# Summing one modulation block on VectorE ahead of the input projection of a two-layer diffusion block

## The chip, the cores and the metric

One core of one Trainium2 chip runs the whole kernel. The metric is the device time of one launch in microseconds (us), the median over several runs.

## The reference

Two layers work on 512 latent tokens and 256 context tokens of width 1024. Each layer normalises the tokens, scales and shifts them with a modulation made from a conditioning vector, mixes them (layer 0: windowed attention beside a gated linear attention; layer 1: neighbourhood attention), adds the result through a modulated gate, and does the same around a feed-forward part. What the change touches is the modulation:

```python
ml = (jax.nn.silu(c) @ w_mod[i] + b_mod[i])[:, None, :]
mc = jax.nn.silu(c_ctx) @ w_mod[i] + b_mod[i]
sh1, sc1, gt1, sh2, sc2, gt2 = jnp.split(ml, 6, axis=-1)
csh1, csc1, cgt1, csh2, csc2, cgt2 = jnp.split(mc, 6, axis=-1)
```

Per layer there are six blocks of 1024 columns, so twelve blocks in all, each a product of two vectors (`c` and `c_ctx`, after SiLU) with a 1024x1024 matrix. Block 2 is `gt1` of layer 0, the gate behind the first mixer. It is not needed before that mixer's output is added.

## The kernel before

All products are in fp32 split into a high and a low part (three matmuls for one). Every engine runs its own hand-ordered list of instructions; semaphores join them.

**Weights.** A weight unit is 128x1024 (512 KB) or less. SyncE (SP) loads units in order into a ring `w_raw` of three; ScalarE rounds each to `w_hi` (L841), GpSimd (POOL) subtracts to get `w_lo` (L526), TensorE multiplies. The first units are `v0` (six units: four for the value columns, whose product has eight steps k = 0 to 7, two steps a unit, and two smaller 640-column ones for 160 further columns), then `in0` (thirteen units, the other columns of the input projection, each half for latent and context tokens). SP also issues, at fixed places between units, the loads of modulation rows.

**Modulation rows.** `m` counts rows of 128x1024 of `w_mod`: m = 8b + k is input block k of modulation block b. Each is a 512 KB load. Blocks 0 and 1 (m = 0 to 15) are finished before or during the first `v0` steps. For m < 40 TensorE does the product itself: `modulation_rows` (L1796) waits for the landing of row m and does four matmuls of 128x32 by 128x256, one to each group of 32 partitions; the 32 matmuls of a block show as 64 records. For m >= 40 (blocks 5 to 11) VectorE does it: `add_rows` (L1288 for k = 0, L1291 for the others) multiplies a row by the scalar of each of two vectors ("lanes") and adds it to an accumulator of 128x1024 each, and TensorE then sums over partitions once (`modulation_sum`, L1811), four matmuls a lane. `mod_used` counts rows done by TensorE, `mod_acc` VectorE's operations, `mod_summed` the sums. After either, ScalarE copies the block out of PSUM (`mod_copy`, L853) and TensorE turns it (`modulation_columns`, L1823).

**Places.** Rows m = 16 to 23 (block 2) lie in the eight slots of `mod_early`; rows 24 to 29 take slots 2 to 7 again, so each of these loads waits until its slot was read. Rows 30 to 33 lie in `gate_b[:, 1]`, `xs[:, 0]`, `xs[:, 1]` and `full`. `xs` is also the scratch of the step that makes `h_lo` (L1459, L1466), and would be the accumulator of block 2.

**The order around the change.** SP issues rows 16 to 23 ahead of the last `v0` unit. Ahead of the second `in0` unit (`in0` + 1) it waits until the tokens are ready and loads rows 30 to 33; ahead of the fourth (`in0` + 3) it loads rows 24 to 29, each behind its slot's wait. VectorE, after making `h_lo` and two mask copies (`window_b`, `near_b`), waits for the end of all `v0` products, and then copies `r_tok` and `a_v` out of PSUM. TensorE turns `r_tok` (L2040), VectorE copies the result to `r_t` (L1494, L1495), TensorE meanwhile does the rows of block 2 and then `gla_z` (L2052), which needs `r_t`. Then come the thirteen `in0` units (L1722). In the middle and at the end of each, `in0_step` inserts small work: in the middle of the first rows 24 to 26, two `gla_z` and the columns of block 2; at its end rows 27 to 29; in the second rows 30 to 33. The first five places are

```python
rows = {(0, 0): 3, (0, 1): 3, (1, 0): 2, (1, 1): 2, (2, 0): 2, (2, 1): 2, (3, 0): 2}
```

where (i, 0) is the middle and (i, 1) the end of unit i. `claim` makes TensorE wait until a PSUM bank was read.

Of the kernel before, what the change touches and what calls it, by code (L numbers as in the profile page):

```python
# [187 lines left out]
def late_rows():  # L188

    steps = {(("fi0L", 0), j): [36 + 2 * j, 37 + 2 * j] for j in range(2, 11)}  # L190
    steps |= {(("fo0L", 0), n): [58 + 2 * n, 59 + 2 * n] for n in range(6)}
    steps |= {(("fi0L", 1), j): [70 + 2 * j, 71 + 2 * j] for j in range(9)}
    steps |= {(("fi1L", 0), j): [86 + 2 * j, 87 + 2 * j] for j in range(1, 5)}
    order = list(steps)
    loads = {at: steps[then] for at, then in zip(order, order[1:])}
    loads[("fi0L", 0), 1] = [40, 41]
    loads[("fi1L", 0), 0] = [88, 89]
    del loads[("fi0L", 1), 8]
    return steps, loads
# [38 lines left out]
def build(nc, a, out):  # L238
# [14 lines left out]
    def sp(name):  # L253
        return start[name]
# [7 lines left out]
    with ExitStack() as ctx:  # L262
# [177 lines left out]
        def gate_load(eng, j):  # L440
            eng.wait_ge(gate_out, 16 * (j + 1))
            if j == 1:
                eng.wait_ge(mod_summed, 5)
            if gb_after[j]:
                eng.wait_ge(post_n, gb_after[j])
            else:
                eng.wait_ge(gl_o, NT)
            rows, n = gate_rows[j], 2 if j < 2 else 1
            eng.dma_start(gate_b[:, 0:n], bass.AP(rows.tensor, rows.offset, [[0, P], [D, n], [1, D]]))\
                .then_inc(gate_in, 16)  # L450
# [24 lines left out]
        def lanes(b):  # L475
            return 2 if b < 8 else 1

        def sums_done(m):
            return sum(lanes(x // KT) for x in range(MOD_LATE, m + 1))

        def sum_place(b, lane):
            return (gate_b if b in (6, 8, 9) else xs)[:, 1 if b == 9 else lane, :]
# [1 line left out]
        def mod_load(eng, m):  # L484
            if m >= MOD_LATE:
                if mod_free(m):
                    eng.wait_ge(mod_acc, sums_done(mod_free(m) - 1))
                if m in (43, 91):
                    eng.wait_ge(pre_lo, PRE["mix1"] if m == 43 else PRE["ffn1L"] + LT)
            elif mod_free(m):  # L490
                eng.wait_ge(mod_used, mod_free(m))
            b, k = divmod(m, KT)
            l, i = divmod(b, 6)
            if m < 2 * KT:
                both = a["w_mod"][0, k * P:(k + 1) * P, 0:2 * D].rearrange("p (i h n) -> p i h n", i=2, h=2)
                eng.dma_start(mod_place(m).rearrange("p (i n) -> p i n", i=2), both[:, :, b])\
                    .then_inc(mod_landing(m)[0], 16)
                return
            eng.dma_start(mod_place(m), a["w_mod"][l, k * P:(k + 1) * P, i * D:(i + 1) * D])\
                .then_inc(mod_landing(m)[0], 16)  # L500
# [139 lines left out]
        @block.sync  # L640
        def _(sync):
            sync.dma_start(ident[:], a["k_ident"]).then_inc(ident_in, 16)
            sync.dma_start(par_rows[0:96, 0, :], a["b_mod"].rearrange("l (r n) -> (l r) n", n=P)).then_inc(par_in, 16)
            at = 0
            for name in ("g_mix_pre", "g_mix_post", "g_ffn_pre", "g_ffn_post", "gla_norm_g"):
                src = a[name].rearrange("l (r n) -> (l r) n", n=P)
                n = src.shape[0]
                sync.dma_start(par_rows[at:at + n, 1, :], src).then_inc(par_in, 16)
                at += n
            for src in (a["c"].rearrange("b (r n) -> (b r) n", n=P), a["c_ctx"].rearrange("(r n) -> r n", n=P)):  # L650
                sync.dma_start(par_rows[at:at + KT, 1, :], src).then_inc(par_in, 16)
                at += KT
            sync.dma_start(sink[:], a["a_sink"].partition_broadcast(P)).then_inc(par_in, 16)
            for m in range(KT):
                mod_load(sync, m)
            for u, parts in enumerate(units):
                if u in (sp("v0") + 1, sp("v0") + 2):
                    first = KT + 4 * (u - sp("v0") - 1)
                    for m in range(first, first + 4):
                        mod_load(sync, m)  # L660
                if u == sp("v0") + RAW:
                    for dst, src in ((mask_in[:, 0:LT * 2 * P], a["k_near"]), (mask_in[:, LT * 2 * P:], a["k_window"]),
                                     (tri[:].rearrange("p a n -> p (a n)"), a["k_tri"])):
                        sync.dma_start(dst, src).then_inc(consts_in, 16)
                if u == sp("v0") + RAW + 2:
                    for m in range(2 * KT, 3 * KT):
                        mod_load(sync, m)
                if u == sp("in0") + 1:
                    sync.wait_ge(pre_lo, PRE["mix0"] + NT)
                    sync.wait_ge(mod_turned, 2)  # L670
                    for m in range(3 * KT + 6, 3 * KT + 10):
                        mod_load(sync, m)
                if u == sp("in0") + 3:
                    for m in range(3 * KT, 3 * KT + 6):
                        mod_load(sync, m)
                if u == sp("in0") + 11:
                    sync.wait_ge(gl_q, NT)
                    sync.wait_ge(gl_k, NT)
                    for dst, src in ((cos, a["k_cos"]), (sin, a["k_sin"])):
                        sync.dma_start(dst, src).then_inc(rope_in, 16)  # L680
                if u == sp("out0L") + RAW:
                    gate_load(sync, 0)
                if u >= RAW:
                    sync.wait_ge(w_hi_done, u - RAW + 1)
                    sync.wait_ge(*low_ready(u - RAW))
                for layout, at, width, src in parts:
                    dst = w_raw[{"top": slice(0, 64), "bottom": slice(64, P)}.get(layout, slice(0, P)), u % RAW, :]
                    if layout == "fm":
                        dst = dst.rearrange("p (k n) -> p k n", k=KT)
                        dst = dst[:, :, at:at + width]  # L690
                    elif layout == "four":
                        dst = dst[:, 0:4 * VR].rearrange("p (k n) -> p k n", k=4)[:, :, at:at + width]
                    else:
                        dst = dst[:, at:at + width]
                    sync.dma_start(dst, src).then_inc(landed[u % RAW], 16)
            for t in L_TILES:
                sync.wait_ge(post_x, POST["fo1L"] + t + 1)
                sync.dma_start(out[0, t * P:(t + 1) * P, :], x_res[:, t, :]).then_inc(stored, 16)
            sync.wait_ge(stored, 16 * LT)
# [122 lines left out]
        def _(act):  # L822
# [21 lines left out]

            def mod_copy(b):

                if b < 5:
                    act.wait_ge(mod_used, KT * (b + 1))
                else:
                    act.wait_ge(mod_summed, b - 4)  # L850
                if b >= 2:
                    act.wait_ge(mod_turned, b - 1)
                act.activation(row_place(b), ps(mod_bank(b), 0, 256), ACT.Copy).then_inc(mod_copied, 1)  # L853
# [338 lines left out]
        def _(dve):  # L1192
            def pre_scale(name, i, tiles):
                n = PRE[name] + i
                dve.wait_ge(pre_rs, n + 1)
                if name == "mix1":
                    dve.wait_ge(mod_summed, 6)
                if n >= 2:
                    dve.wait_ge(pre_tr, n - 1)
                dve.tensor_scalar(xs[:, n % 2, :], x_res[:, tiles[i], :], rs_pre[:, n:n + 1], None,  # L1200
                                  ALU.mult).then_inc(pre_xs, 1)
# [73 lines left out]

            def add_rows(at):

                free = {5: (pre_tr, PRE["mix1"]), 6: (post_n, POST["fo0L"]), 7: (mod_summed, 1), 8: (mod_summed, 2),
                        9: (mod_summed, 2), 10: (mod_summed, 3), 11: (pre_tr, PRE["ffn1L"] + LT)}
                for m in late_steps.get(at, ()):  # L1280
                    b, k = divmod(m, KT)
                    dve.wait_ge(*mod_landing(m))
# [201 lines left out]
            dve.wait_ge(consts_in, 16 * 3)  # L1484
            dve.tensor_copy(window_b[:], mask_in[:, LT * 2 * P:])
            dve.tensor_copy(near_b[:].rearrange("p t n -> p (t n)"), mask_in[:, 0:LT * 2 * P]).then_inc(masks_done, 1)
            dve.wait_ge(w_used, sp("v0") + KT // 2 + 2)
            rows = [ps(6 + b, 0, 3 * VR).rearrange("p (t n) -> p t n", t=3) for b in range(2)]
            for b in range(2):
# [211 lines left out]
        def _(pe):  # L1701
# [339 lines left out]
                               r_tok[:, t, :], ident[:], start=True, stop=True)  # L2041
            mm.then_inc(r_turned, 1)
            read_by((2, 6), (r_in, 1))
            modulation_rows(range(2 * KT, 3 * KT))

            def gla_z(n):
                bank, t = 4 + n % 2, GLA_TILES[n]
# [215 lines left out]
```

## Time and profile before

| | us |
|---|---|
| median of 3 runs | 1747.09 |
| lowest, highest | 1743.4, 1752.45 |
| profiled execution, whole | 1751.41 |
| its span | 1749.6 |
| TensorE matmul busy | 1677.9 (96%) |
| VectorE busy | 709.6 (41%) |
| ScalarE busy | 641.9 (37%) |
| GpSimd busy | 678.1 (39%) |

The span is the stretch of the profile in which the engines work; the whole time is 1.8 us more. Matmuls overlap in the pipeline, so a group's busy time is not their sum. All times of the trace are us from the start of the span.

### The profile page before, as it was taken

The numbers are of one execution on the slowest core, as the hardware profiler recorded it, in microseconds if no ns is written. First come the engines' busy times: TensorE is split into PE (matmuls) and PEld (weight loads), VectorE is DVE, ScalarE is ACT, GpSimd is POOL, SyncE is SP. The second block draws the span as 40 slices with busy tenths as digits, with TensorE's granted clock in tenths as the row PEclk, the third lists the DMA queues.
The fourth block names the chain that finished last, engine by engine and source line by source line (L and its number), as shares of the span: only waits on it lengthen the run. The fifth ranks groups of instructions, "written<-read, shape, count | busy, mean of one in ns | idle before, by whom it ended". The sixth has DMA issues, their size and how long they took to land.

```text
span 1749.6 us, 25876 instructions
## 1 busy us (share of the span) xinstructions
PE 1677.9 (96%) x10242; PEld 1397.5 (80%) x10242; DVE 709.6 (41%) x1124; ACT 641.9 (37%) x1118; POOL 678.1 (39%) x454
## 2 busy tenths in 40 slices
PE   6999999999999999999899999999999999999997
PEld 4868887777877887878899878877887888888886
DVE  5135547707589635403455420015771451011103
ACT  4242126726422122213555342236762522222221
POOL 3211222038455545433542043335433444444443
PEclk9999999999999999999999999999999999999999
DMA  9553101023465645524556636432002353333331
GB/s 356 182 169 85 38 25 49 1 81 115 146 188 192 229 145 182 167 87 118 154 160 183 193 107 116 91 98 95 2 2 61 100 165 97 105 90 97 98 98 67
DMA packets 211987, 207.17 MB, mean 118 GB/s; under 512 B 16262, under 2 KB 180636, under 8 KB 211612
## 3 DMA queue, kind: packets, MB, share of 16 engines
q1 hardware_dynamic: 199208, 165.53, 31.6%
q10 hardware_dynamic: 12660, 39.99, 7.4%
q8 instruction: 82, 1.34, 0.3%
q14 instruction: 37, 0.30, 0.1%
HBM read 203.37 MB, written 2.13 MB: 117 GB/s over the span
## 4 chain that ended last, share of the span: by engine, by line
PE 82%; DVE 5%; issue 4%; ACT 4%; POOL 4%; DMA 1%; SPq 0%; ACTq 0%; POOLq 0%; DVEq 0%
PE ps L1722 38%; PE ps L1749 26%; PE ps L1900 3%; POOL w_lo L526 3%; PE ps L1956 3%; PE ps L2016 3%; PE ps L1921 3%; ACT w_hi L841 2%; PE ps L1796 1%; PE ps L1835 1%; DVE xs L1291 1%; DMA w_raw<-in_w_ffn_in 1%; PE ps L1968 1%; DVE hid_f L1310 1%; DMA mod_early<-in_w_mod 1%
## 5 line engine op out<-in xcount | busy, mean ns | idle before, releaser
L526 POOL TENSOR_TENSOR w_lo<-w_raw,w_hi 128x1024 fp32r<-128x1024 f32 (+1 forms) x221 | 558.5, 2529 | 892.4 <-ACT w_hi L841 892.2
L1722 PE MATMUL ps<-h_hi,w_hi 128*128 128x512 f32 (+1 forms) x1488 | 496.9, 352 | 11.9 <-POOL w_lo L526 8.1
L1722 PE MATMUL ps<-h_hi,w_lo 128*128 128x512 f32 (+1 forms) x1488 | 492.4, 349 | 0.0
L1722 PE MATMUL ps<-h_lo,w_hi 128*128 128x512 f32 (+1 forms) x1488 | 491.2, 349 | 0.0
L841 ACT ACTIVATE w_hi<-w_raw 128x1024 fp32r<-128x1024 f32 (+1 forms) x273 | 286.6, 1051 | 346.0 <-PE ps L1749 312.0
L1722 PEld LDWEIGHTS ps<-h_hi,w_hi 128*128 128x128 f32 x1488 | 269.9, 189 | 56.9 <-issue 20.8
L1722 PEld LDWEIGHTS ps<-h_hi,w_lo 128*128 128x128 f32 x1488 | 269.5, 189 | 36.1
L1722 PEld LDWEIGHTS ps<-h_lo,w_hi 128*128 128x128 f32 x1488 | 269.5, 189 | 35.7
L526 DVE TENSOR_TENSOR w_lo<-w_raw,w_hi 128x1024 fp32r<-128x1024 f32 x52 | 69.3, 1335 | 201.7 <-ACT w_hi L841 198.8
L1749 PE MATMUL ps<-w_hi,hid_hi 128*128 128x512 f32 x440 | 137.0, 393 | 8.0 <-ACT mod_row L853 4.2
L1310 DVE TENSOR_TENSOR hid_f<-silu_g,ps 128x512 f32<-128x512 f32 (+1 forms) x66 | 39.3, 595 | 254.2 <-PE ps L1722 253.8
L1749 PE MATMUL ps<-w_lo,hid_hi 128*128 128x512 f32 x440 | 136.1, 391 | 0.0
L1749 PE MATMUL ps<-w_hi,hid_lo 128*128 128x512 f32 x440 | 136.1, 391 | 0.0
L912 ACT ACTIVATE hid_hi<-hid_f 128x512 fp32r<-128x512 f32 (+1 forms) x66 | 37.0, 560 | 252.2 <-DVE hid_f L1310 252.2
L1749 PEld LDWEIGHTS ps<-w_hi,hid_hi 128*128 128x128 f32 x440 | 82.6, 189 | 27.0 <-issue 10.2
L1749 PEld LDWEIGHTS ps<-w_lo,hid_hi 128*128 128x128 f32 x440 | 83.1, 189 | 17.4
L1749 PEld LDWEIGHTS ps<-w_hi,hid_lo 128*128 128x128 f32 x440 | 82.9, 188 | 17.3
L1749 PE MATMUL ps<-w_hi,h_hi 128*128 128x512 f32 x256 | 81.9, 402 | 10.6 <-POOL w_lo L526 3.4
L941 ACT ACTIVATE prob<-prob,negm 128x512 f32<-128x512 f32 (+2 forms) x112 | 78.1, 699 | 27.1 <-DVE negm L1350 18.4
L908 ACT ACTIVATE silu_g<-ps 128x512 f32<-128x512 f32 (+1 forms) x66 | 34.5, 523 | 144.5 <-PE ps L1722 144.4
L1749 PE MATMUL ps<-w_lo,h_hi 128*128 128x512 f32 x256 | 81.1, 399 | 0.0
L1749 PE MATMUL ps<-w_hi,h_lo 128*128 128x512 f32 x256 | 80.4, 396 | 0.0
(223 smaller groups left out, 1898.8 us busy)
## 6 DMA issues: line engine op xcount, KB each, us to landing
w_raw<-in_w_ffn_in SPq DMA_DIRECT2D x132, 512.0 KB, 3.8
w_raw<-in_w_ffn_out SPq DMA_DIRECT2D x66, 512.0 KB, 3.5
mod_raw<-in_w_mod ACTq DMA_DIRECT2D x42, 512.0 KB, 4.5
w_raw<-in_na_w_in SPq DMA_DIRECT2D x32, 512.0 KB, 3.7
mod_early<-in_w_mod SPq DMA_DIRECT2D x30, 512.0 KB, 9.8
full<-in_w_mod ACTq DMA_DIRECT2D x15, 512.0 KB, 5.1
w_raw<-in_ab_w_in SPq DMA_DIRECT2D x18, 256.0 KB, 5.9
w_raw<-in_ab_w_in SPq DMA_DIRECT2D x9, 512.0 KB, 8.9
```

Of the source, the lines that this page charges most:

```text
L526: eng.tensor_tensor(w_lo[:, u % RING, 0:width], w_raw[:, u % RAW, 0:width], w_hi[:, u % RING, 0:width].bitcast(F32), ALU.subtract).then_in ...
L841: act.activation(w_hi[:, u % RING, 0:width], w_raw[:, u % RAW, 0:width], ACT.Copy).then_inc(w_hi_done, 1)
L908: act.activation(silu_g[:, f % 2, 0:width], ps(2 * (f % 2), 0, width), ACT.Silu)\
L912: act.activation(hid_hi[:, j * width:(j + 1) * width], hid_f[:, f % 2, 0:width], ACT.Copy)\
L941: act.activation(prob[:, p % 2, x, 0:n], prob[:, p % 2, x, 0:n], ACT.Exp, bias=negm[:, c % 2, head:head + 1], scale=SCALE if layer == 0 el ...
L1310: dve.tensor_tensor(hid_f[:, f % 2, 0:width], silu_g[:, f % 2, 0:width], ps(2 * (f % 2) + 1, 0, width), ALU.mult).then_inc(ff_full, 1)
L1722: mm = pe.matmul(o[0], sta(x, o), mov(y, o), start=first and n == 0, stop=last and n == 2)
L1749: mm = pe.matmul(o, act(x, k, t), w[y][:, c:c + n], start=k == 0 and (x, y) == ("hi", "hi") and first_in_bank(name, i, c), stop=k == n_uni ...
L1900: mm = pe.matmul(ps(scores_bank(layer, p, x), at, at + width), q, kk[:, col:col + width], start=at % 512 == 0, stop=i == len(runs[x]) - 1, ...
L1921: mm = pe.transpose(ps(4 + x, j * P, (j + 1) * P), probs(p, x, j), ident[:])
L1956: mm = pe.matmul(ps(bank, at, at + P, 64 * x, 64 * x + 64), value_tile(p, x, j), turned_probs(layer, p)[:, x, j * P:(j + 1) * P], start=j ...
L2016: mm = pe.matmul(place(t), h_act(x, k, t), w[y][:, at:at + width], start=k == 0 and (x, y) == ("hi", "hi") and (first or t in (0, 3)), sto ...
```

## The change

Block 2 goes over to VectorE. Its accumulation stands in VectorE's list between the two mask copies and the wait for the end of the `v0` products, TensorE does `modulation_sum(2)` where it did the 32 row matmuls, and the loads of rows 30 to 33 move in SP's list from ahead of `in0` + 1 to ahead of `in0` + 2, behind a wait for that sum, since two of them write where the accumulators lie. The loads of rows 24 to 29 stay ahead of `in0` + 3. The counts that waits use are adapted.

```diff
@@ late_rows
     order = list(steps)
+    steps["v0"] = list(range(2 * KT, 3 * KT))
     loads = {at: steps[then] for at, then in zip(order, order[1:])}
@@ gate_load
-                eng.wait_ge(mod_summed, 5)
+                eng.wait_ge(mod_summed, 6)
@@
+        def by_sums(m):
+            return m // KT == 2 or m >= MOD_LATE
+
         def sums_done(m):
-            return sum(lanes(x // KT) for x in range(MOD_LATE, m + 1))
+            return sum(lanes(x // KT) for x in range(m + 1) if by_sums(x))
+
+        def rows_done(m):
+            return sum(not by_sums(x) for x in range(m + 1))
@@ mod_load
             elif mod_free(m):
-                eng.wait_ge(mod_used, mod_free(m))
+                prev = mod_free(m) - 1
+                eng.wait_ge(*(mod_acc, sums_done(prev)) if by_sums(prev) else (mod_used, rows_done(prev)))
@@ sync
-                if u == sp("in0") + 1:
+                if u == sp("in0") + 2:
                     sync.wait_ge(pre_lo, PRE["mix0"] + NT)
                     sync.wait_ge(mod_turned, 2)
+                    sync.wait_ge(mod_summed, 1)
                     for m in range(3 * KT + 6, 3 * KT + 10):
                         mod_load(sync, m)
                 if u == sp("in0") + 3:
@@ mod_copy
-                if b < 5:
-                    act.wait_ge(mod_used, KT * (b + 1))
+                if b < 5 and b != 2:
+                    act.wait_ge(mod_used, rows_done(KT * (b + 1) - 1))
                 else:
-                    act.wait_ge(mod_summed, b - 4)
+                    act.wait_ge(mod_summed, max(1, b - 3))
@@ pre_scale
-                    dve.wait_ge(mod_summed, 6)
+                    dve.wait_ge(mod_summed, 7)
@@ add_rows
-                free = {5: (pre_tr, PRE["mix1"]), 6: (post_n, POST["fo0L"]), 7: (mod_summed, 1), 8: (mod_summed, 2),
-                        9: (mod_summed, 2), 10: (mod_summed, 3), 11: (pre_tr, PRE["ffn1L"] + LT)}
+                free = {2: (pre_lo, NT), 5: (pre_tr, PRE["mix1"]), 6: (post_n, POST["fo0L"]), 7: (mod_summed, 2),
+                        8: (mod_summed, 3), 9: (mod_summed, 3), 10: (mod_summed, 4), 11: (pre_tr, PRE["ffn1L"] + LT)}
@@ vector
             dve.tensor_copy(near_b[:].rearrange("p t n -> p (t n)"), mask_in[:, 0:LT * 2 * P]).then_inc(masks_done, 1)
+            add_rows("v0")
             dve.wait_ge(w_used, sp("v0") + KT // 2 + 2)
@@ tensor
             read_by((2, 6), (r_in, 1))
-            modulation_rows(range(2 * KT, 3 * KT))
+            modulation_sum(2)
```

## Rows read from the trace of the kernel before

**Rows 1.** The page's first line.
```profile
span 1749.6 us, 25876 instructions
```

**Rows 2.** Chain that ended last, in time order: start, us, what; 90 to 111 us.
```profile
90.51 1.36 PE ps L2040 x11
91.87 3.56 PE ps L1796 x62
95.43 1.91 PE ps L2052 x4
97.34 4.36 PE ps L1722 x24
101.71 1.43 PE ps L1796 x24
...
105.42 4.24 PE ps L1722 x24
109.66 1.43 PE ps L1796 x24
```

**Rows 3.** Timeline of VectorE, 60 to 93 us: start, us, instruction, idle before.
```profile
60.46 0.69 DVE L1486 CAST near_b<-mask_in 128x1024 bf16<-128x1024 f32 x1
89.01 0.42 DVE L1490 COPY r_tok<-ps 128x96 f32<-128x96 f32 x2 [27.87 <-PE ps L2016]
...
92.62 0.40 DVE L1495 COPY r_t<-ps 32x256 f32<-32x256 f32 x1
```

**Rows 4.** Timeline of SP's DMA issues: rows 16-23, 24-29, then a weight unit.
```profile
40.58 7.92 SPq L499 DMA_DIRECT2D mod_early<-in_w_mod  x8
...
93.35 2.96 SPq L499 DMA_DIRECT2D mod_early<-in_w_mod  x6
...
96.94 3.81 SPq L695 DMA_DIRECT2D w_raw<-in_ab_w_in  x1
```

**Rows 5.** Issue to landing: `mod_early`, 40-49 and 93-98 us; the unit of 96.94.
```profile
DMA to landing us min/median/max: 5.4/7.5/9.2
...
DMA to landing us min/median/max: 3.7/7.0/8.9
...
w_raw<-in_ab_w_in SPq DMA_DIRECT2D x1, 512.0 KB, 11.5
```

**Rows 6.** Timeline of TensorE at a later block's sum, two lanes.
```profile
511.05 1.07 PE L1811 MATMUL ps<-xs,one_hot 128*32 128x256 f32 x16 [0.79 <-DVE xs L1291]
```

**Rows 7.** Timeline of VectorE, 465 to 560 us: accumulation of a later block.
```profile
468.78 3.55 DVE L1288 TENSOR_SCALAR xs<-mod_raw,c_pad 128x1024 f32<-128x1024 f32 x2
472.25 2.47 DVE L1291 SCALAR_TENSOR_TENSOR xs<-mod_raw,c_pad,xs 128x1024 f32<-128x1024 f32 x2
...
479.65 4.61 DVE L1291 SCALAR_TENSOR_TENSOR xs<-mod_raw,c_pad,xs 128x1024 f32<-128x1024 f32 x2
```

**Rows 8.** Timeline of GpSimd, some of 59 to 89 us, and one at 480 us.
```profile
59.02 4.38 POOL L526 TENSOR_TENSOR w_lo<-w_raw,w_hi 128x1024 fp32r<-128x1024 f32 x1 [15.79 <-ACT w_hi L841]
...
66.00 1.57 POOL L526 TENSOR_TENSOR w_lo<-w_raw,w_hi 128x640 fp32r<-128x640 f32 x1 [1.08 <-ACT w_hi L841]
...
82.17 2.38 POOL L526 TENSOR_TENSOR w_lo<-w_raw,w_hi 128x1024 fp32r<-128x1024 f32 x1 [5.62 <-ACT w_hi L841]
...
480.04 3.14 POOL L526 TENSOR_TENSOR w_lo<-w_raw,w_hi 128x1024 fp32r<-128x1024 f32 x1 [3.07 <-ACT w_hi L841]
```

**Rows 9.** Timeline of ScalarE at the end of the sixth `v0` step.
```profile
65.18 0.74 ACT L841 ACTIVATE w_hi<-w_raw 128x640 fp32r<-128x640 f32 x1 [5.62 <-PE ps L2016]
```

**Rows 10.** Windows: length, busy (count) of PE, PEld, DVE, ACT, POOL, then PEclk, DMA, GB/s.
```profile
88.99:92.00 3.01, 1.49 (x19) 1.49 (x23) 1.35 (x4) 0.00 (x0) 0.00 (x0) 1.00 0.00 0
...
348.70:352.70 4.00, 2.03 (x26) 1.43 (x26) 2.33 (x7) 2.32 (x6) 0.00 (x0) 1.00 0.00 2
352.70:356.10 3.40, 3.17 (x8) 2.52 (x9) 0.00 (x0) 0.47 (x1) 2.37 (x1) 0.50 0.02 5
...
1366.50:1369.90 3.40, 2.18 (x9) 2.11 (x10) 3.13 (x6) 2.17 (x3) 1.26 (x2) 0.50 0.02 7
1369.90:1373.30 3.40, 3.40 (x9) 2.70 (x8) 1.20 (x4) 1.34 (x4) 1.77 (x1) 0.50 0.06 16
```

## The prediction

> **What bounds the kernel now.** The page gives the frame: a span of 1749.6 us [rows 1], which with the 1.8 us around it is the 1751.4 us of the profiled execution; that is 4.3 us over the median of 1747.1. I work out a difference on the profile's own times and put it on the median.
>
> I then read the chain of waits in order of time around the work that changes. From 90.5 us on it lies on TensorE alone: turning `r_tok`, the rows of block 2 (3.56 us), `gla_z`, half of the first `in0` unit, rows 24 to 26, and so on [rows 2]. So each us that TensorE gains or loses here moves the end by as much, unless a wait for another engine or for a DMA opens.
>
> The timeline of VectorE comes next, because the new work goes there. It finishes `near_b` at 61.15 (60.46 + 0.69) and does nothing until 89.01, where the end of the `v0` products lets it copy `r_tok`; a hole of 27.9 us. Its last copy to `r_t`, which `gla_z` needs, ends at 93.02 (92.62 + 0.40) [rows 3]. Last, the queue of SP with the time from issue to landing: rows 16 to 23 are issued from 40.58 to 48.5, and the longest takes 9.2 us, so all are there before 57.7. Rows 24 to 29 are issued from 93.35 to 96.3, each when TensorE has read its slot, followed by the weight units of `in0` + 3 and + 4 [rows 4, 5].
>
> **The change, part by part.**
>
> *TensorE's product.* Removed: 32 matmuls (64 records), 3.56 us [rows 2]. Added: 8 matmuls, 16 records; such a sum took 1.07 us from its first start to its last end at 511 us [rows 6], and at the pace of the row matmuls (3.56 / 62 = 0.057 us a record) it is 0.92. Starting at 91.87 the sum ends near 92.8. `gla_z` could follow, but `r_t` is ready only at 93.02, so it starts at about 93.05 instead of 95.43. Gain: 2.4 us (bounds 2.0 if the semaphore takes 0.4 us more, 2.6 if nothing but the sum counted). This wait costs 0.25 us and is new.
>
> *VectorE's accumulation.* Added: two operations of the L1288 kind and fourteen of the L1291 kind. A pair of the latter takes 2.47 us undisturbed, 4.61 us when a GpSimd subtraction falls into it; the GpSimd operation of 480.04 then takes 3.14 instead of 2.38 us [rows 7, 8]. So a pair loses 2.14 us to each full unit. For the pair of L1288, 3.55 - 2.14 = 1.41 undisturbed [rows 7]. Work: 1.41 + 7 x 2.47 = 18.7 us. GpSimd has five units in the hole: the one of 59.02 (until 63.4), two of 640 columns (the first of them right behind it, the second at 66.00), and those of 74.17 (like the next) and 82.17 [rows 8]. With 2.14 for a full unit and 1.3 for a 640-column one (1.57 less the share 0.9 = 2.14/2.38, rounded down) the loss is 3 x 2.14 + 2 x 1.3 = 9.0. The end is 61.15 + 18.7 + 9.0 = 88.9 us, just before `r_tok` wants the engine at 89.01. I take no delay; bounds: 6.5 us early, if the GpSimd operations fell only beside dead time, and 1.5 us late.
>
> The Trainium skill's page "SBUF — State Buffer", section "Who interferes with whom", says that a VectorE operation with two SBUF inputs, or in a two-port mode, and a GpSimd operation shut each other out for the whole instruction. The disturbed pair agrees in kind, but lost 2.14 us and not the full 2.38. By the page's rule the loss would be 3 x 2.38 + 2 x 1.57 = 10.3 us and VectorE would end at 90.1, 1.1 us late; by the row it is on time.
>
> *The other side of it.* The `w_lo` of the fourth `v0` unit is done at 63.4. It is used in the seventh `v0` step, which begins just before 65.18, where ScalarE is released by the end of the sixth [rows 9]: at about 64.9. One VectorE operation in front of it costs GpSimd 0.76 us (3.14 - 2.38), which fits into the 1.5 us. I take nothing; two more would cost TensorE up to 1 us. The 640-column unit behind it is needed only after two more steps.
>
> *SP's queue.* This is the costly part. The loads of rows 30 to 33 used to go out during the `v0` products, alone, and had landed long before use. They now wait for the sum: 92.8 us and some 0.13 for the semaphore (row 24 used to be issued 0.13 us after its slot was free), so 92.95. SP takes its list in order, and behind that wait stand the weight unit `in0` + 2, then rows 24 to 29, then `in0` + 3 and + 4. The early reading of `mod_early` by VectorE does not help rows 24 to 29, because SP stands in front of them. Before, row 24 was the first of a burst; now five 512 KB loads are ahead of it. In the burst of before, the first load landed at 93.35 + 3.7 = 97.05, the sixth (row 29) at about 95.9 + 8.9 = 104.8, the eighth (`in0` + 4) at 96.94 + 11.5 = 108.44 [rows 4, 5]. That is 1.55 us a load up to the sixth and 1.63 up to the eighth; the eighth lands 15.1 us after the first issue. In the new order row 24 is sixth, row 25 seventh, row 26 eighth. At the pace of the rows (3.7 + 7 x 1.55 = 14.55) rows 24, 25, 26 land at about 104.4, 105.9 and 107.5. Bounds for the last: 105.95 (as if the weight unit ahead cost nothing, 13.0) and 108.5 (15.1, and half a us for SP).
>
> TensorE would ask for row 24 at 93.05 + 1.91 + 4.36 = 99.3 [rows 2]. It waits 5.3 us, does each row as it comes, and has finished row 26 at 107.5 + 0.48 (a third of 1.43) = 107.95. Before, the same point was 101.71 + 1.43 = 103.14 [rows 2]. Loss against before: **4.8 us**, with the 2.4 us gained already in it (bounds 3.3 and 5.8). Rows 27 to 29 land by 107.5 + 3 x 1.55 = 112.2; TensorE asks for them at 109.66 + 4.8 = 114.4, so there is no second wait. Unit `in0` + 2 lands as the fifth, near 103, and is needed after two whole `in0` units, past 118; `in0` + 3 lands near 113.8, and ScalarE comes to it only after the end of the first unit, 109.66 + 4.8 = 114.5. Both are covered.
>
> *TensorE's clock.* After a stretch in which TensorE was busy 2.03 of 4.0 us the granted clock fell to 0.50 (1.2 GHz) for 3.4 us, at 352.7; at 1366.5 it stayed there for two such stretches, 6.8 us, the first of them busy only 2.18 us [rows 10]. With 1.5 of 3.0 us busy around 89 us it did not fall [rows 10]. The new stretch, 99.3 to 107.9, has some 1.4 us of work in 8.6: less than before either fall. So I expect a fall. It costs half of the time that TensorE works at it: 1.7 us for 3.4 us, up to 3.4 us for 6.8; part of it is spent waiting, so I take 2.4 (bounds 0 and 3.4).
>
> *The rest* (counts in the other waits, `mod_copy(2)` earlier by some 2.5 us, places of the later blocks) moves nothing that is late.
>
> Sum: 4.8 + 2.4 = +7.2 us, in the profile's terms 1751.4 + 7.2 = 1758.6, on the median 1747.1 + 7.2 = **1754.3 us** (+0.4%).
>
> **The rivals.**
>
> *The rows come in time.* If loads did not land in the order of issue, or the queue drained faster than 0.4 us a load, there would be no wait at 99.3 and the gain of 2.4 us remains: 1744.7. For it: nothing else is being loaded then. Against it: in the burst of before the first load landed 3.7 us, the sixth 11.5 us and the eighth 15.1 us behind the first issue. It decides if row 26 lands before 99.3, 6.4 us after SP's wait ends.
>
> *Late rows, but the clock holds.* +4.8: 1751.9. For it: there are three small bursts of rows in the gap. Against it: the falls of before came after less idling.
>
> *Worse in every queue.* Row 26 at the upper bound (+1), VectorE 1.5 us late, a stall of 1 us in the seventh step and the clock at half for 6.8 us (+1): about +11.5, 1758.6. The mechanism that would do it is VectorE overrunning 89.01, since that moves `r_tok`, the sum, SP's wait and the rows together; beyond 1.5 us of overrun the total is over +8.7. The rule of the page "SBUF — State Buffer" of the Trainium skill would give 1.1 us of that overrun, +8.3 in all, 1755.4.
>
> *Every accumulation slow.* If all sixteen ran beside GpSimd as in the disturbed pairs, 8 x 4.61 = 36.9 us from 61.15 would end at 98.0, 9 us late: +16. Only five GpSimd units exist in the hole, which speaks against it.
>
> **How the numbers follow.** About 0.5% (8.7 us) is what a measurement of this kernel can tell from no change. Chances: forecast (late rows and a clock fall, +6 to +9) 0.50; late rows without a fall 0.20; worse in every queue 0.15; rows in time 0.12; all slow 0.03. The three runs of before spread over 9 us, so the median of a few may be off by 2 to 3. Slower by over 0.5%: a quarter of the forecast, most of the two worse cases, 0.29. Faster by over 0.5% needs the rival of -2.4 and a low draw: 0.02. Within: 0.69. The range reaches from the rows in time (1744.7) to somewhat beyond the worse case: 1745 to 1761.
>
> **What would show each step.** In the profile after: sixteen L1288 and L1291 operations from 61.2 to about 89, and `r_tok` at 89.0; L1811 at 91.9 for 1 us; `gla_z` near 93; the four loads issued by SP from about 92.95, followed by a weight unit and then rows 24 to 29; TensorE idle from 99.3 on "DMA mod_early", row 26 done near 107.9; a stretch of half clock behind it; from there on everything later by the same amount. I am wrong if the idle is missing or under 3 us, if VectorE ends after 90.5, or if a later wait swallows the shift.

## The result, and the profile after

| | before | after |
|---|---|---|
| median of 6 runs | 1749.07 us | 1758.11 us |
| lowest, highest | 1743.4, 1752.45 | 1756.52, 1761.5 |
| span of the profiled execution | 1749.6 us | 1756.6 us |

The ratio is 1.0059 (95% interval 1.004 to 1.0078): slower by 7 to 14 us. The forecast was +7.2 us, 1754.3, with 1758.1 inside the range. Three more runs of the kernel before put its median at 1749.07 where the forecast had started from 1747.09; between the two medians above lie 9.0 us.

VectorE first. Its timeline in the changed kernel (start us, us, instruction, idle before) answers to [rows 3]:

```profile
60.16 0.69 DVE L1495 CAST near_b<-mask_in 128x1024 bf16<-128x1024 f32 x1
60.76 4.86 DVE L1297 TENSOR_SCALAR xs<-mod_early,c_pad 128x1024 f32<-128x1024 f32 x2
65.54 22.39 DVE L1300 SCALAR_TENSOR_TENSOR xs<-mod_early,c_pad,xs 128x1024 f32<-128x1024 f32 x14
88.71 0.42 DVE L1500 COPY r_tok<-ps 128x96 f32<-128x96 f32 x2 [0.78 <-PE ps L2026]
```

The sixteen operations fill the hole and end at 87.93, 0.78 us before `r_tok` is due. `r_tok` itself starts at 88.71 against 89.01 before; it starts between 87.7 and 89.3 in the profiles of this study, at 88.74 and 87.95 in two executions of one kernel, so stages are best measured from here.

The chain in order of time (start, us, what) answers to [rows 2]:

```profile
90.21 1.36 PE ps L2050 x11
91.57 1.04 PE ps L1821 x13
92.61 0.02 issue
92.62 0.03 SPq L679
92.65 0.03 issue
92.68 0.34 SPq L507
...
97.36 9.10 DMA mod_early<-in_w_mod
106.46 0.04 issue
106.50 1.08 PE ps L1806 x8
107.58 3.71 PE ps L2062 x4
111.29 0.62 PE ps L1833 x2
111.91 6.33 PE ps L1732 x24
118.24 1.43 PE ps L1806 x24
```

Behind the turning of `r_tok` the chain leaves TensorE, which it did not do in the kernel before [rows 2]: from the sum (L1821) it goes to SP, through the issues of the four loads that waited for it, a weight unit and rows 24 and 25, then the 9.1 us from the issue of row 26 to its landing. The timeline of SP shows the order of the queue, and answers to [rows 4]:

```profile
92.68 0.34 SPq L507 DMA_DIRECT2D gate_b<-in_w_mod  x1
93.07 0.90 SPq L507 DMA_DIRECT2D xs<-in_w_mod  x2
94.01 0.43 SPq L507 DMA_DIRECT2D full<-in_w_mod  x1
94.54 0.61 SPq L704 DMA_DIRECT2D w_raw<-in_ab_w_in  x1
95.20 4.29 SPq L507 DMA_DIRECT2D mod_early<-in_w_mod  x6
```

What TensorE waits for shows in its own timeline:

```profile
104.02 2.28 PE L1806 MATMUL ps<-mod_early,c_pad 128*32 128x256 f32 x16 [4.76 <-DMA mod_early<-in_w_mod]
106.50 1.08 PE L1806 MATMUL ps<-mod_early,c_pad 128*32 128x256 f32 x8 [0.20 <-DMA mod_early<-in_w_mod]
```

4.76 us of waiting for row 24, then the rows one by one as they land. The windows of the same stretch (columns as in [rows 10]) show the clock:

```profile
98.90:102.90 4.00, 0.36 (x3) 0.04 (x1) 0.00 (x0) 0.28 (x1) 0.00 (x0) 0.99 1.06 338
102.90:106.50 3.60, 2.17 (x17) 0.43 (x17) 0.00 (x0) 0.78 (x1) 2.35 (x1) 0.50 1.02 416
106.50:111.90 5.40, 5.40 (x15) 2.05 (x16) 0.00 (x0) 0.00 (x0) 0.00 (x0) 0.50 1.09 363
111.90:116.60 4.70, 4.70 (x17) 3.98 (x16) 2.92 (x6) 0.00 (x0) 0.00 (x0) 0.52 0.72 178
116.60:120.00 3.40, 3.40 (x35) 2.15 (x34) 0.00 (x0) 1.72 (x3) 0.00 (x0) 1.00 0.00 0
```

The clock falls to half at 102.9 and is back at 116.6, 13.7 us later, though TensorE has worked without a break since 106.5. After the first rows TensorE does the same work as before in more time: `gla_z` 3.71 us against 1.91, the columns 0.62 against 0.37, half a unit 6.33 against 4.24 [rows 2]; together +4.1 us. The stage ends where the state products begin (L2084 before, L2094 after). The rows of these lines (durations in ns, first and last start in us) put them at 157.1 in the kernel before, 68.1 us behind `r_tok`, and at 165.7 in the changed one:

```profile
L2084 PE MATMUL ps<-b_v,kg_t x176: 268/270/321, 157.1 to 185.2; 64*64 64x128 f32 x176
L2094 PE MATMUL ps<-b_v,kg_t x176: 268/270/321, 165.7 to 193.8; 64*64 64x128 f32 x176
```

That is 77.0 us behind `r_tok`. So the stage is 8.9 us longer: 4.74 us until row 26 is done (107.58 - 88.71 = 18.87 against 103.14 - 89.01 = 14.13), and 4.14 of half clock behind it. The first part has some half clock in it too: row 26 alone took 1.08 us, where a single row takes 0.64 at full clock (in the run with 11 filling matmuls below), so of the 8.9 us some 4.3 are late rows and 4.6 the clock.

The span grew by only 7.0. The last operation of L941 (L950 in the changed kernel) starts at 1305.2 before and 1314.9 after, 9.7 us later; the last table load of L908 (L917) at 1379.0 and 1385.9, 6.9 us later. Between the two the kernel before has its 6.8 us at half clock (1366.5 to 1373.3 [rows 10]), and the changed one, in this execution, has no such stretch. That fits the 2.8 us; half clock far behind the change comes and goes from one execution to the next (the second profile of the kernel with rows first has such stretches near 268 and 351 us, the first has none there), and the stage is the better measure of the change.

### The profile page after: what moved, and what is told of

The parts are those of the page before. It is cut to its first block, busy times and chain, and to the rows that moved or that the text cites. A ratio compares the mean times of both kernels' runs of the same rounds, so it can differ in the third digit from the quotient of the medians.

```text
span 1756.6 us, 25804 instructions
## 1 busy us (share of the span) xinstructions
PE 1678.5 (96%) x10194; PEld 1395.1 (79%) x10194; DVE 733.6 (42%) x1140; ACT 642.2 (37%) x1118; POOL 679.9 (39%) x454
## 4 chain that ended last, share of the span: by engine, by line
PE 84%; DVE 5%; issue 4%; POOL 3%; ACT 3%; DMA 1%; SPq 1%; ACTq 0%; DVEq 0%; POOLq 0%
PE ps L1732 40%; PE ps L1759 26%; PE ps L1910 3%; PE ps L2026 3%; PE ps L1966 3%; POOL w_lo L534 2%; PE ps L1931 2%; DMA mod_early<-in_w_mod 1%; PE ps L1845 1%; ACT w_hi L850 1%; PE ps L1806 1%; DVE xs L1300 1%; PE ps L2121 1%; PE ps L1978 1%; DVE full L1249 1%
## 5 line engine op out<-in xcount | busy, mean ns | idle before, releaser
L1759 PEld LDWEIGHTS ps<-w_lo,hid_hi 128*128 128x128 f32 x440 | 83.4, 189 | 17.5
L950 ACT ACTIVATE prob<-prob,negm 128x512 f32<-128x512 f32 (+2 forms) x112 | 78.2, 699 | 28.5 <-DVE negm L1359 19.6
L917 ACT ACTIVATE silu_g<-ps 128x512 f32<-128x512 f32 (+1 forms) x66 | 34.5, 523 | 145.1 <-PE ps L1732 144.8
```

The source lines that it names most:

```text
L917: act.activation(silu_g[:, f % 2, 0:width], ps(2 * (f % 2), 0, width), ACT.Silu)\
L950: act.activation(prob[:, p % 2, x, 0:n], prob[:, p % 2, x, 0:n], ACT.Exp, bias=negm[:, c % 2, head:head + 1], scale=SCALE if layer == 0 el ...
L1759: mm = pe.matmul(o, act(x, k, t), w[y][:, c:c + n], start=k == 0 and (x, y) == ("hi", "hi") and first_in_bank(name, i, c), stop=k == n_uni ...
```

## The experiments

Seven runs of six kernels were made, in two sets, each beside the kernel before. The table sets the times beside the stage, `r_tok` to first state product, from each profile; the ratio of the changed kernel is that of the result above.

| kernel | ratio to before (95%) | `r_tok` | first state product | stage |
|---|---|---|---|---|
| before | | 89.01 | 157.1 | 68.1 |
| changed | 1.0059 (1.0040 to 1.0078) | 88.71 | 165.7 | 77.0 |
| rows 24 to 29 first | 1.0002 (0.9988 to 1.0016) | 88.74 | 154.6 | 65.9 |
| the same again | 0.9987 (0.9972 to 1.0002) | 87.95 | 153.8 | 65.9 |
| move of the loads alone | 1.0077 (1.0058 to 1.0096) | 87.67 | 168.7 | 81.0 |
| one weight unit less ahead | 1.0046 (1.0028 to 1.0063) | 88.48 | 163.0 | 74.5 |
| wait filled, 22 matmuls | 1.0053 (1.0033 to 1.0073) | 87.74 | 163.2 | 75.5 |
| wait filled, 11 matmuls | 1.0020 (1.0005 to 1.0035) | 87.77 | 161.4 | 73.6 |
| rows first, other PSUM bank | 0.9975 (0.9961 to 0.9989) | 89.27 | 154.2 | 64.9 |

### Rows 24 to 29 ahead of the wait

The edit is against the changed kernel. The weight unit `in0` + 2 goes ahead of the wait too.

```diff
-                if u == sp("in0") + 2:
+                if u == sp("in0") + 3:
+                    for m in range(3 * KT, 3 * KT + 6):
+                        mod_load(sync, m)
                     sync.wait_ge(pre_lo, PRE["mix0"] + NT)
                     sync.wait_ge(mod_turned, 2)
                     sync.wait_ge(mod_summed, 1)
                     for m in range(3 * KT + 6, 3 * KT + 10):
-                        mod_load(sync, m)
-                if u == sp("in0") + 3:
-                    for m in range(3 * KT, 3 * KT + 6):
                         mod_load(sync, m)
```

> The changed kernel with the loads of rows 24 to 29 moved ahead of the wait for the sum and of rows 30 to 33 (all ten ahead of in0 + 3). Theory (rows 24 to 26 land late because SP stands at the wait for the sum, and the clock falls in the idle this makes): rows 24 to 29 are issued between 67 and 88 us as VectorE frees their slots, there is no wait at 99 us, no stretch at half clock before 300 us, and rows 24 to 26 are done at 99.0 + 1.4 = 100.4 to 100.8 instead of 107.6 (103.1 in the kernel before); time 2.4 us under the kernel before, about 1746.7. Rival (the work on VectorE, or its sharing with GpSimd, costs the time): still slower than the kernel before by 5 us or more.

Measured: the timeline of SP has the six rows while VectorE accumulates, and the four others behind the sum:

```profile
71.77 16.55 SPq L507 DMA_DIRECT2D mod_early<-in_w_mod  x6
92.71 0.33 SPq L507 DMA_DIRECT2D gate_b<-in_w_mod  x1
```

and the chain stays on VectorE and TensorE, with no DMA in it:

```profile
92.42 0.34 DVE r_t L1504
92.76 0.14 issue
92.90 1.95 PE ps L2061 x4
94.85 4.43 PE ps L1731 x24
99.29 1.43 PE ps L1805 x24
100.72 1.91 PE ps L2061 x4
```

Rows 24 to 26 are done at 100.72, the first stretch at half clock behind them is at 400.2 us, and the stage is 65.9 us: 2.2 shorter than before and 11.1 shorter than in the changed kernel. VectorE did the same sixteen operations (22.40 us for the fourteen) and ended at the same place. So the work on VectorE costs nothing here; the order of the loads cost the stage all that it lost. The timed gain over the kernel before, 0.14% expected, is not resolved by this set (1.0002, 0.9988 to 1.0016).

### The same again

> The kernel with rows 24 to 29 first once more, unchanged, for a second profile and more timed runs: theory: first state product 2.4 us earlier than in the kernel before, and a time 2.4 us (0.14%) under it, which the first set of runs neither showed nor excluded clearly (ratio 1.0002, 0.9988 to 1.0016). Rival: the gain of the stage is given back later, so that the span is that of the kernel before.

Measured: 0.9987 (0.9972 to 1.0002), stage 65.9 again, spans 1745.9 and 1747.4 against 1749.6. The stage's gain is in both profiles and both spans are shorter; the two sets of times lie around -0.05% together. The interval of this set holds -0.14%, that of the first ends just short of it at -0.12%, and both hold no change. So the gain is shown in the stage, and not in the time; whether a part of it is given back later is open.

### The move of the loads alone, without VectorE's work

The edit is against the kernel before.

```diff
-                if u == sp("in0") + 1:
+                if u == sp("in0") + 2:
                     sync.wait_ge(pre_lo, PRE["mix0"] + NT)
                     sync.wait_ge(mod_turned, 2)
+                    sync.wait_ge(mod_used, 3 * KT)
```

> The kernel before with only the move of the loads of rows 30 to 33: ahead of in0 + 2, behind a wait until TensorE has done block 2's rows (mod_used 24). No accumulation on VectorE. Theory (late loads): SP's burst starts at 95.5, row 26 lands 14.6 us later at 110.1, TensorE has asked since 101.7 and is done at 110.6 instead of 103.1: +7.4 us, and about +4 us for half clock as in the changed kernel: 11 to 12 us slower than the kernel before. Rival (the work on VectorE costs the time): within 2 us of the kernel before.

Measured: 1.0077, 13.5 us slower; the stage 12.9 us longer, and the wait for the rows in TensorE's timeline is longer than in the changed kernel:

```profile
108.21 2.27 PE L1797 MATMUL ps<-mod_early,c_pad 128*32 128x256 f32 x16 [7.84 <-DMA mod_early<-in_w_mod]
110.67 1.08 PE L1797 MATMUL ps<-mod_early,c_pad 128*32 128x256 f32 x8 [0.20 <-DMA mod_early<-in_w_mod]
```

The rival falls: the kernel is slower with nothing added to VectorE. The size is 1 to 2.5 us over what was expected, as row 26 was done 17.5 us after the first issue of the burst (94.23 to 111.76) and not 14.9 as in the changed kernel (92.68 to 107.58), for the same eight loads. The chains show where the 2.6 us lie: row 26 is issued 7.1 us behind the first load (101.33) against 4.7 (97.36), and lands 9.3 us after its issue against 9.1. Two issues by SP took longer, 1.35 us where it was 0.43 and 3.32 where it was 1.60. What held SP is open. The clock was at half for 13.7 us here too.

### One weight unit less ahead of the rows

Against the changed kernel, the wait and all ten loads stand ahead of `in0` + 3, still rows 30 to 33 first.

```diff
-                if u == sp("in0") + 2:
+                if u == sp("in0") + 3:
                     sync.wait_ge(pre_lo, PRE["mix0"] + NT)
                     ...
                     for m in range(3 * KT + 6, 3 * KT + 10):
                         mod_load(sync, m)
-                if u == sp("in0") + 3:
                     for m in range(3 * KT, 3 * KT + 6):
                         mod_load(sync, m)
```

> The changed kernel with the wait and the loads of rows 30 to 33 ahead of in0 + 3, so that the weight unit in0 + 2 is issued early, at about 68 us, and row 26 is the seventh load of the burst and not the eighth. Theory: row 26 lands 1.5 us earlier, rows 24 to 26 done at about 106.0 instead of 107.6, still at half clock for some 13 us; 1.5 us faster than the changed kernel, 7 to 8 us slower than the kernel before. Rival (the number of loads in front does not set the landing): no earlier landing.

Measured: rows 24 to 26 done at 105.52, 17.04 us after `r_tok` against 18.87, so 1.8 us less for one load less; half clock for 10.2 us, where some 13 were expected; the stage 2.5 us shorter; ratio 1.0046 against 1.0059, intervals overlapping, so the gain over the changed kernel is shown in the stage alone. One load less in front of the rows brought their landing forward by 1.8 us, and the burst of the kernel before has 1.55 to 1.63 us a load [rows 4, 5].

### The wait filled with work for TensorE

Against the changed kernel; `...` stands for the entry of `fill` in the table of the steps.

```diff
+    steps[0, 0] = [("busy", 22)]
     for at, n in rows.items():
@@
+            def fill(n):
+                claim(7)
+                keep_busy(7, n)
...
```

> The changed kernel with 22 dummy matmuls of 128x256 (0.22 us each) on TensorE in front of rows 24 to 26, into the PSUM bank that these rows then overwrite; they fill most of the 5 us wait. Theory (the idle makes the clock fall, which costs 4.1 us): rows 24 to 26 are still done at about 107.6, no stretch at half clock around 103 to 116 us, and the stage is 4 us shorter than in the changed kernel; 4 to 5 us slower than the kernel before. Rival (the clock falls for another reason, or the fall costs nothing): same as the changed kernel.

Measured: a miss in size. The timeline of TensorE shows the filling (22 matmuls, 44 records):

```profile
98.13 9.66 PE L2008 MATMUL ps<-x_res,ident 128*128 128x256 f32 x44
107.72 1.50 PE L1807 MATMUL ps<-mod_early,c_pad 128*32 128x256 f32 x24
```

I had taken a record for a matmul; the filling took 9.5 us and outlasted the wait by over 2 us. The clock did hold (1.00 in every window from 96 to 120), the rows were finished at 109.22, 21.5 us behind `r_tok` instead of 18.9, and still the stage was 1.5 us shorter than in the changed kernel: 2.6 us lost, 4.1 us gained from the clock. The times cannot tell the two kernels apart (1.0053 against 1.0059). With 11 matmuls:

> The changed kernel with 11 dummy matmuls in front of rows 24 to 26 instead of 22: in the run with 22 they took 9.5 us (0.43 us each, not 0.22), longer than the wait they were to fill, so 11 take 4.7 us. Theory (idle makes the clock fall and that costs 4.1 us of the change): rows 24 to 26 done within 0.5 us of where the changed kernel has them, no or only a short stretch at half clock before 300 us, the first state product (kg_t, L2084 in the kernel before) starts 4 us earlier than in the changed kernel, about 161.5; 4 to 5 us slower than the kernel before. Rival (the fall does not matter, or comes anyway): the first state product at 165.7 as in the changed kernel.

```profile
98.14 4.91 PE L2008 MATMUL ps<-x_res,ident 128*128 128x256 f32 x22
102.98 0.64 PE L1807 MATMUL ps<-mod_early,c_pad 128*32 128x256 f32 x8
104.01 0.64 PE L1807 MATMUL ps<-mod_early,c_pad 128*32 128x256 f32 x8 [0.39 <-DMA mod_early<-in_w_mod]
105.29 0.64 PE L1807 MATMUL ps<-mod_early,c_pad 128*32 128x256 f32 x8 [0.64 <-DMA mod_early<-in_w_mod]
```

Measured: the waits are now 0.4 and 0.6 us, half clock only from 107.8 for 3.4 us instead of 13.7, the stage 73.6 us: 3.4 shorter than in the changed kernel although row 26 lands only 0.3 us sooner (17.5 us behind `r_tok` against 17.75), and 1.0020 (1.0005 to 1.0035) of the time before. So it is shown that the idle brought on the long half clock, and that this made a part of the loss: 3.1 us of the 3.4 came back with it. Of the 5.5 us that remain, 4.0 are late rows (done 18.2 us behind `r_tok`, 14.1 before) and 1.5 are the half clock that is left (0.57 us for the columns and 5.55 for half a unit, against 0.37 and 4.24).

### Another bank for the turned `r_tok`

On top of the first experiment; the line with the matmul is shortened at `...`:

```diff
-            claim(2, 6)
+            claim(0, 2)
             for t in range(NT):
-                mm = pe.matmul(ps(*(6, t * P, (t + 1) * P) if t < LT else ...
+                mm = pe.matmul(ps(*(0, t * P, (t + 1) * P) if t < LT else ...
@@
-            dve.tensor_copy(r_t[0:32, 0:SEQ], ps(6, 0, SEQ, 0, 32))
+            dve.tensor_copy(r_t[0:32, 0:SEQ], ps(0, 0, SEQ, 0, 32))
@@
-            read_by((2, 6), (r_in, 1))
+            read_by((0, 2), (r_in, 1))
```

> The kernel with rows 24 to 29 first, and r_tok turned into PSUM bank 0 instead of bank 6, so that TensorE need not wait until VectorE has copied a_v out of banks 6 and 7. Expected: the turning starts 0.9 us earlier (right behind the r_tok copies), gla_z 0.5 to 0.9 us earlier, the first state product at 153.7 to 154.1 (154.6 with rows first, 157.1 before); 3.0 to 3.4 us faster than the kernel before, 0.2%. Rival (the a_v copies only move behind and delay the r_t copies by as much): no gain over rows first.

Measured: the chain has lost the `a_v` copies:

```profile
89.27 0.43 DVE r_tok L1499 x2
89.70 0.04 issue
89.75 1.39 PE ps L2049 x11
91.13 0.12 PE ps L1820
91.26 0.02 issue
91.28 0.68 DVE r_t L1503
91.96 0.34 DVE r_t L1504
92.30 0.14 issue
92.44 1.95 PE ps L2061 x4
```

`gla_z` starts 3.17 us behind `r_tok` instead of 4.16, the stage is 64.9 us, 3.2 less than before. The ratio is 0.9975 (0.9961 to 0.9989), so this version is faster than both kernels: by 2 to 7 us than before, and by about 9 us or more than the changed one if the two ratios are set side by side. That it is faster than the version with rows first is shown by the stage (1.0 us); the intervals of the two ratios overlap.

## Why the prediction was right

**TensorE's product.** Forecast: sum 91.87 to 92.8, `gla_z` at 93.05. Measured: 91.57 to 92.61 (1.04 us against 0.92), `gla_z` at 92.87, behind a wait of 0.33 us for `r_t`. Counted from `r_tok`, 4.16 us against 6.42 before: a gain of 2.26 (forecast 2.4). The runs with rows first show that it stays, 2.2 us of stage, when nothing follows it.

**VectorE.** Forecast: end at 88.9. Measured: 87.93. Some 0.4 us of the difference is the earlier start (60.76), and 0.5 was counted twice in the work:

```profile
77.35 3.67 DVE L1300 SCALAR_TENSOR_TENSOR xs<-mod_early,c_pad,xs 128x1024 f32<-128x1024 f32 x3
74.03 3.40 DVE L1300 SCALAR_TENSOR_TENSOR xs<-mod_early,c_pad,xs 128x1024 f32<-128x1024 f32 x1
73.87 2.47 POOL L534 TENSOR_TENSOR w_lo<-w_raw,w_hi 128x1024 fp32r<-128x1024 f32 x1 [5.63 <-ACT w_hi L850]
```

Undisturbed, three operations take 3.67 us and a pair 2.47 [rows 7], so one starts every 1.20 us and 1.27 passes until the last ends; seven pairs of 2.47 count the overlap of neighbours each time. By starts the work is about 18.2 us and not 18.7 (estimate: 14 x 1.20, 1.33 for the pair of L1297, 0.07 for the last end), and of the 27.2 us from 60.76 to 87.93 some 9.0 are lost beside GpSimd, as forecast.

The Trainium skill's page "SBUF — State Buffer", section "Who interferes with whom", calls the shared ports an exclusive lock; the prediction made 10.3 us of loss and an end at 90.1 of it. The disturbed operation agrees with the lock: it ends at 77.43, 1.09 us behind GpSimd's at 76.34, less than an undisturbed one takes from start to end, so it got next to nothing done beside it. The sum was too large, as each GpSimd operation was counted whole. GpSimd took 6.35, 2.53, 2.47 and 2.59 us where it had 5.90, 1.57, 2.38 and 2.38; no unit of weights came late for it.

**SP's queue.** The step that decides held. Forecast: burst from 92.95, row 26 done at 107.95, 4.8 us behind the kernel before. Measured: 92.68, 107.58, and 4.74 us counted from `r_tok`. That the two agree so closely is luck: row 26 landed 13.8 us behind the first issue (92.68 to 106.46) and not 14.55, and its product then took 1.08 us at half clock and not 0.48. That the order of the loads is the cause, and not the work on VectorE, is shown from both sides: the move alone is slower (+12.9 us of stage), the work without the bad order is not (-2.2 us). Rows 27 to 29 and the weight units brought no second wait, as forecast.

**The clock.** Right in kind, mis-sized: the forecast took 2.4 us (bounds 0 and 3.4) for one or two stretches of 3.4 us at half clock; it was one of 13.7 us and cost 4.14 us behind row 26, and some 0.4 us in that row, more than the upper bound. The rows of before that it was sized by show the clock back after 3.4 to 6.8 us [rows 10]. Here it stayed at half for 10.1 us after TensorE had resumed without a further break, through `gla_z` and the columns and half a unit, with 15 matmul records in 5.4 us. What in this work kept it down was not tried. Behind row 26 the term is 1.7 us too small, which is the difference between the forecast +7.2 and the stage's +8.9; the +9.0 of the medians agrees, and the interval of +7 to +14 holds both.

**The rivals.** "The rows come in time" did not come about by itself but is what the reordered kernel makes true: 2.2 of its 2.4 us in the stage, not resolved in the time. "Late rows, but the clock holds" (+4.8) is nearly the run filled with 11 matmuls: +5.5 in the stage with 1.5 of half clock in it, +3.5 in time. VectorE did not overrun, and not every accumulation was slow. The measured +0.59% lies beyond the 0.5% bound, on the side that had 0.29.

## What to carry to other kernels

A wait put into a DMA queue delays everything behind it: before moving a load behind a later event, list what stands behind it in that queue, and let the loads that are wanted first go first. Here taking six loads and a weight unit out from behind the wait turned +8.9 us in the stage into -2.2. When TensorE's wait is one that idles it for some us, look in the trace for a half clock behind it and count it as a loss of its own; here it was about as large as the wait's. And when a freed stretch shows a new limit (here copies of `a_v` that shared a bank with what TensorE waited for), look at the banks: the change of one was worth 1.0 us of stage, beside 2.2 for the work taken away.

## What the runs showed of the hardware that was not expected

The half clock outlasted the idle by 10.1 us of uninterrupted matmuls (102.9 to 116.6 us, work again from 106.5); in the two other kernels whose rows came late and unfilled it lasted 13.7 and 10.2 us in all, and at the later falls in the profiles of the kernel before and the changed one 3.4 or 6.8. After 4.9 us of filling and two waits of 0.4 and 0.6 us the clock still fell, for 3.4 us, at 107.8, 2.5 us after the last wait had ended.

Most issues of a 512 KB load by SP in these bursts took 0.33 to 0.68 us, but that of row 24, the sixth load, took 1.60 us in the changed kernel and 3.32 in the run with the move alone; [rows 4] has one of 3.81 for the eighth. In the run with the move alone the loads behind came later for it. What holds SP there these runs do not show.
